# A mixer of two scans in rounds: one shared order of steps becomes a list for each engine

## The reference, cut to what matters

```python
def step(S, inp):                       # RWKV, in each head
    w_t, k_t, v_t, kk_t, a_t = inp[:5]
    sa = jnp.einsum('bhvk,bhk->bhv', S, kk_t)
    S = (S * w_t[:, :, None, :] - sa[..., None] * (kk_t * a_t)[:, :, None, :]
         + v_t[..., None] * k_t[:, :, None, :])
    ...
g = jnp.cumsum(lf_c, axis=2)            # HGRN, in chunks
inter = jnp.einsum('bhtk,bhkv->bhtv', q_c * jnp.exp(g), S)
...
mixed = concat(pool, rwkv, hgrn) * silu(gates);  out = layer_norm(ALPHA * x + gate * (mixed @ w_out))
```

## Time and profile before

| | us |
|---|---|
| median of 3 executions | 1521.52 |
| lowest, highest | 1518.86, 1522.16 |
| the profiled execution: its own time | 1515.97 |
| its span in the trace | 1514.1 |
| tail's last product to the block's last product | 189.1 to 507.6 |

### The profile page before, as it was taken

The page is one execution under the profiler, slowest core; times in us unless marked ns, Lnnn a source line. Parts: engine busy times, 40 slices in busy tenths (PEclk is TensorE's granted clock), DMA queues, the critical chain, the costliest instruction groups (busy, mean ns, idle before and its releaser), DMA issues.

```text
span 1514.1 us, 31114 instructions
## 1 busy us (share of the span) xinstructions
PE 1436.9 (95%) x13535; PEld 1289.6 (85%) x13535; DVE 825.7 (55%) x1495; ACT 332.2 (22%) x688; POOL 281.1 (19%) x144
## 2 busy tenths in 40 slices
PE   5999988997979899999999999999999999999998
PEld 2777877876868798998888999999999888899986
DVE  2345366557353467667435666534767743566643
ACT  1104034235332420143300120002014330012100
POOL 3403210000000047743100000003874310000000
PEclk8899999998999999999999999999999999999999
DMA  9533011102011454433344444445443334444451
GB/s 360 183 112 111 1 31 31 29 4 57 2 59 57 141 191 156 168 112 112 112 167 154 156 172 171 171 140 176 171 167 112 112 112 167 154 156 172 160 183 53
DMA packets 107479, 191.30 MB, mean 126 GB/s; under 512 B 8744, under 2 KB 25856, under 8 KB 107216
## 3 DMA queue, kind: packets, MB, share of 16 engines
q1 hardware_dynamic: 105968, 187.39, 35.3%
q10 hardware_dynamic: 448, 0.66, 0.3%
q0 software_dynamic: 928, 1.26, 0.2%
HBM read 187.32 MB, written 1.05 MB: 124 GB/s over the span
## 4 chain that ended last, share of the span: by engine, by line
PE 87%; DVE 3%; DMA 2%; issue 2%; DVEq 2%; ACT 1%; POOLq 1%; ACTq 1%; POOL 0%; SPq 0%
PE psum L1486 17%; PE psum L1347 14%; PE psum L1322 12%; PE psum L1483 6%; PE psum L1625 5%; PE psum L1606 4%; PE psum L1343 3%; PE psum L900 3%; PE psum L1538 2%; PE psum L974 2%; PE psum L983 2%; PE psum L1142 2%; PE psum L1198 2%; DMA arena<-in_mod_w 1%; PE psum L1407 1%
## 5 line engine op out<-in xcount | busy, mean ns | idle before, releaser
L1347 PE MATMUL psum<-arena 128*128 128x128 f32 x2240 | 262.9, 277 | 2.5 <-DVE arena L2652 1.3
L1347 PEld LDWEIGHTS psum<-arena 128*128 128x128 f32 x2240 | 255.6, 193 | 11.4 <-issue 8.0
L2057 ACT ACTIVATE arena<-psum 128x512 f32<-128x512 f32 (+5 forms) x248 | 118.3, 493 | 662.1 <-PE psum L1347 109.3
L1486 PEld LDWEIGHTS psum<-arena 128*128 128x128 f32 x2240 | 250.4, 192 | 0.1
L1486 PE MATMUL psum<-arena 128*128 128x128 f32 x2240 | 250.5, 275 | 0.0
L1322 PE MATMUL psum<-arena 128*128 128x256 f32 x896 | 195.6, 379 | 0.0
L1322 PEld LDWEIGHTS psum<-arena 128*128 128x128 f32 x896 | 169.5, 190 | 24.4 <-issue 0.3
L855 POOL TENSOR_TENSOR arena<-arena 128x1024 f32<-128x1024 f32 x12 | 28.4, 2371 | 376.6 <-DMA arena<-in_w_in 359.6
L1483 PE MATMUL psum<-arena 128*128 128x256 f32 x448 | 97.0, 379 | 0.0
L1483 PEld LDWEIGHTS psum<-arena 128*128 128x128 f32 x448 | 85.1, 190 | 11.6
L1625 PE MATMUL psum<-arena 128*128 128x256 f32 x336 | 73.5, 380 | 1.1 <-issue 1.1
(11 more groups left out here) (403 smaller groups left out, 2032.8 us busy)
## 6 DMA issues: line engine op xcount, KB each, us to landing
arena<-in_w_in SPq DMA_DIRECT2D x31, 2048.0 KB, 8.2
arena<-in_w_up SPq DMA_DIRECT2D x16, 2048.0 KB, 8.3
arena<-in_w_down SPq DMA_DIRECT2D x16, 2048.0 KB, 7.8
arena<-in_w_out SPq DMA_DIRECT2D x6, 2048.0 KB, 7.7
arena<-in_w_branch SPq DMA_DIRECT2D x6, 2048.0 KB, 7.9
arena<-in_mod_w SPq DMA_DIRECT2D x5, 2048.0 KB, 14.7
arena<-in_w_in SPq DMA_DIRECT2D x12, 512.0 KB, 4.0
arena<-in_w_in SPq DMA_DIRECT2D x3, 1024.0 KB, 6.6
```

The lines of the kernel that those rows point to most:

```text
L1347: mm = pe.matmul(b[:, n * P:(n + 1) * P], left[:, k, n * P:(n + 1) * P], right[:, k, :], start=k == 0, stop=k == half - 1)
L1486: mm = pe.matmul(b[:, n * P:(n + 1) * P], left[:, k, n * P:(n + 1) * P], right[:, k, :], start=first and n == 0 and k == 0, stop=last and ...
L2057: return act.activation(dst, src, ACT.Copy, scale=scale)
```

## The change

`TAIL` and `ROUNDS` go. Each engine gets a list of its own (`ORDERS`, keys P, A and D for TensorE, ScalarE and VectorE), all with the same steps of each stream but interleaved differently. Banks are still given out in TensorE's order; the counts by which an emptied bank is recognised follow the order of the engine that empties it. With it:

- Streams are cut finer: E has 11 steps (the running sums of a direction are two steps), C 12 (u and s apart), G 32 (two k-tiles of a gate tile in each), H 15, V 7.
- In the lists of rounds 0 and 1, VectorE's running sums of the next turn (E.2 to E.5) stand behind the copies of inverse levels 4 to 6, ScalarE's Ln of the key norm behind level 4's first step and its Exp behind level 5's (before, both behind level 6).
- HGRN's whole turn j is done in round j (before, its steps 2 to 7 were done in the chain part of round j-1).
- N and Q have two turns instead of three, heads (0, 1) together and head 2 alone. Both are out of rounds 0 and 1.
- The gate tiles are copied, not passed through Silu; Silu is applied to 128x1024 at once in a stream of its own, Z, at the start of rounds 1 and 2.
- ScalarE copies of levels 1 to 5 only the half of each i product that is used (128x256 for 128x512).
- The inner squares of `xf` are copied at the start of level 6's first step.
- M runs over the tiles in two parts, (2, 3, 5, 6) and then (0, 1, 7), each over all output columns.

```diff
-TAIL = "TTETETEEEEETEETTTHTTTTHE"
-ROUNDS = ("SHSHSHILHVIHVILHVIHVILHVIHLHIEHIEHIEHIEHIEIEECGECGHCGHCGEHCGHCGHCGHCGY",
-          "SSSILHIHILHIHILHIHLIEQNIEQNHIEQNHIEIEQNIEQNEQNCGECGHCGHCGEHCGHCGHCGHCGY",
-          "SSSILHQIHQILHQQIHQILHQIHLIQNIQNIQNIQNQNIQNIMCMCMCMCMCMCMCMCMYMNNMNMNNMMMMN")
+ORDERS = {
+    "P": ("TTETETEEEEEETEETTTHTTTTE",
+          "SSSIHLILHILILHIEHIHEHIVHIHVHIVHIVHIHIHVCVVGGCGCGGHCGCGCGGCGCGCGGCGCGCGEEEEEEEEEY",
+          "SSSIZHLILIHLILHIEHIHEIHIHIHHIHIHIHCGGCGCGGHCGCGCGGHCGCGCGGHCGCGCGEEEEEEEEEY",
+          "SSSIZHLILIHLILHIHINHIQQQHINNHIHHIHIHIQQQNNNHCCMCMHCMCMCHHCMCMCMCMCQQQCYQQQNMMNNMMMNNMMMN"),
+    "A": ("TTETETEEEEEETEETTTHTTTTE",
+          "SSSIHILLHIILLHIEHIHEHIEEEEEVHIHVHIEVHIVHIHIHVCCCVVGGGGGHECCCGGGGECCCGGGGCCCGGGEY",
+          "SSSIZHILLIHILLHIEHIHEIEEEEEHIHIEHHIHIHIHCCCGGGGGHECCCGGGGEHCCCGGGGHCCCGGGEY",
+          "SSSIZHILLIHILLHIQHINHINQQHINHIQNHHIHIQNHIQNHCCCMMHCCCMMHHCCCQMMMCCCMQQQYQQNNMMMMMMMMNNNN"),
+    "D": ("TTETETEEEEEETEETTTHTTTTE",
+          "SSSIHLILHILILHIEHIHEHIVHIHVHEIEVHIVHEIEHIHVCVVCCGGGGGHEECCCGGGGECCCGGGGECCCGGGEY",
+          "SSSIZHLILIHLILHIEHIHEIHIHEIEHHIHEIEHIHCCCGGGGGHEECCCGGGGHECCCGGGGHECCCGGGEY",
+          "SSSIZHLILIHLILHIHIQNHIHINNQQHIHHIHIHIQQQNNNHCCCMMHCCCMMHHCCCQMMMCCCMQQYQQQNNNMMMMMMMMNNN"),
+}
...
+def run_streams(engine, **streams):
+
+    for x, _, _ in order_of_streams(engine):
         next(streams[x])
...
         def inverse_scalar(act, j, copy, done, emptied):
...
                     rw.wait_filled(act, g)
-                    emptied(rw, copy(wh[r, d].rearrange("p u t -> p (u t)"), bank(rw, g)[r]))
+                    if l < 6:
+                        emptied(rw, copy(halves_of(wh[:, d].rearrange("p u t -> p (u t)"), l, d == 0), halves_of(bank(rw, g), l, d == 0)))
+                    else:
+                        emptied(rw, copy(wh[r, d].rearrange("p u t -> p (u t)"), bank(rw, g)[r]))
...
+        def gates_made(act, done):
+
+            for j in range(JT - 1):
+                v = hz[:, j:j + 4:3, :]
+                act.drain()
+                act.activation(v, v, ACT.Silu)
+                done("gates_ready")
+                yield
...
                 dve.tensor_tensor(km[:, d, :], km[:, d, :], k, ALU.mult)
                 fence()
+                yield
                 dve.tensor_tensor(blocks_of(c), blocks_of(c), m.unsqueeze(2).to_broadcast([P, 4, P]), ALU.subtract)
...
+            for part, ks in enumerate(((2, 3, 5, 6), (0, 1, 7))):
+                for n in range(4):
                     w = use_chunk(pe, 12 + n // 2)
```

More of the change, by code:

```diff
@@ L220, in __init__ @@
         self.met = met
+        for engine, order in emptied:
+            for n, g in enumerate([g for g, e, _ in order if e == engine], 1):
+                self.empty[g] = (engine, n)
     def bank(self, g):
@@ L241, in wait_all, with order_of_streams @@
                 eng.wait_ge(self.emptied[e], self.met[e])
[L244 to L254 removed]
+TURNS = {"T": 1, "V": 1, "M": 1, "G": JT - 1, "Z": JT - 1, "Q": 2, "N": 2}
+ORDERS = {
[12 more added lines that the diff above has]
+}
+def order_of_streams(engine):
+    steps, met = [], collections.Counter()
+    for x in "".join(ORDERS[engine]):
         n = len(GROUPS[x])
@@ L917, in prepare_tensor @@
             yield
-            for _ in range(6):
+            for _ in range(8):
                 yield
@@ L1183, in mixed_out_tensor @@
         def mixed_out_tensor(pe):
-            for n in range(4):
-                if n % 2 == 0:
+            for part, ks in enumerate(((2, 3, 5, 6), (0, 1, 7))):
+                for n in range(4):
                     w = use_chunk(pe, 12 + n // 2)
[L1188 to L1196, removed]
+                    if part:
+                        pe.wait_ge(sem("o_mixed"), 2)
+                    elif n == 0:
+                        ep.wait_all(pe)
+                        pe.wait_ge(sem("o_mixed"), 1)
+                        pe.wait_ge(sem("y_mixed"), 1)
+                    elif n == 2:
+                        hg.wait_all(pe)
+                    b = bank(wo, f"wo{n}")
+                    for t in range(2):
+                        c = (2 * (n % 2) + t) * P
                         for k in ks:
-                            pe.matmul(b[:, t * T:(t + 1) * T], w[:, k, c:c + P], mixed[k], start=k == 0 and t == 0, stop=False,
+                            pe.matmul(b[:, t * T:(t + 1) * T], w[:, k, c:c + P], mixed[k], start=k == 2 and t == 0, stop=False,
                                       skip_group_check=True)
@@ L1307, in turns_of, with two_turns_of @@
                 yield from stream(args[0], j, *args[1:])
+        def two_turns_of(stream, *args):
+            for js in ((0, 1), (2,)):
+                yield from stream(args[0], js, *args[1:])
         def layer_tensor(pe, l, take_bank, turn):
@@ L1875, in prepare_scalar @@
             done("e_gates")
-            yield
-            yield
-            yield
+            for _ in range(5):
+                yield
             ep.wait_filled(act, f"kk_{j}")
@@ L2038, in hgrn_scalar @@
             emptied(hg, copy(ktok.rearrange("p d c t -> p (d c t)"), bank(hg, f"ktok_{j}")))
-            for _ in range(5):
+            for _ in range(7):
                 yield
@@ L2452, in inverse_vector @@
             for l in range(1, 7):
+                if l == 6:
+                    if j == 0:
+                        dve.wait_ge(sem("squares_zeroed"), 1)
+                    for d in range(2):
+                        for r in HALVES:
+                            dve.tensor_copy(xf[r, d, :, r], xh[r, d])
                 yield
```

205 lines of the change are left out of this document (114 added, 91 removed).

## The result

The changed kernel is slower. Its median is 1532.9 us against 1517.0 us for the kernel before (20 executions each); the ratio is 1.0092, 95% interval 1.0069 to 1.0114, that is 14 us (the medians differ by 15.9). The forecast was 1516.9 us, 0.30% faster than the 1521.5 that three executions of the kernel before had given; its 20 executions here lie 4.5 us lower, so it is the direction and the difference that count, not the 1516.9. Slower by over 0.2% had a chance of 0.20. The profiled execution has a span of 1531.8 us (before 1514.1) and took 1533.67.

The account below looks back on a forecast made before the run. PE's queue was taken to bound the kernel. Old idle 34.0 + clock 10.8 + matmuls saved 0.9 - new idle 32.8 - new clock loss 8.3 = 4.6 us faster, giving 1516.9 us; range 1505 to 1526.

Parts of the forecast that it names:

- the clock: Time lost to PE's low clock in the rounds of the new kernel, put at 8.3 us.
- PE's new idle time: PE's idle time in the rounds: 10.8, 12.5 and 9.5 us in rounds 0, 1 and 2, in all 32.8.
- kk: The key norm's matmul in rounds 0 and 1, said to wait 0.86 us for ScalarE to empty a bank.
- the price of the sums: Running sums in rounds 0 and 1: PE waits of 4.6 and 7.1 us, plus 6.8 us of clock.
- I followed the three new lists against each other: How new idle time in the rounds was worked out, with durations from the profile rows; 32.8 us in all.
- The queue of 17.8 us has no gap.: VectorE's queue in round 1 from HGRN's level 1, without pause, against PE's 11.0 us; PE waits 7.1.
- the old idle time of 34.0 was all set free: In the rounds, all 34.0 us of PE's old idle time was counted as going.
- two stretches are sure, at 3.4 us each: Low clock behind the waits of 4.6 and 4.7 us; half a chance of another 3.0 behind round 2's 2.2.
- Rival 2: Waits of 1.6 to 2.2 us close together also take the clock down in the rounds; 1525.4 us, chance 0.17.
- Rival 1: Sums in rounds 0 and 1 are hidden and the clock holds; 1500.8 us, or 1505.5 with half the waits; chance 0.20.
- Rival 3: Sums only change places, waits behind them add up to what they were; 0.9 us faster, 1520.6; chance 0.19.
- Rival 4: ScalarE's half copies in the inverse levels save nothing; 0.4 to 1 us more, inside the forecast; no chance given.

Follow-up runs that it names:

- experiment 1: Changed kernel with VectorE's running sums moved behind the chain's state copies in rounds 0 and 1; 1516.3 us, ratio 0.9986 to the kernel before.
- experiment 11: Experiment 8's kernel with the four running-sum steps of VectorE put back where the changed kernel has them; 1525.3 us, ratio 1.0048 to the kernel before.
- experiment 2: Changed kernel with VectorE's growth behind the cross block put ahead of the output block's steps 2 and 3 in round 2; 1526.3 us, ratio 1.0053.
- experiment 5: Changed kernel with HGRN's state step of round 1 behind x of inverse level 5, on TensorE and VectorE; 1527.9 us, ratio 1.0065 to the kernel before.
- the repetition: The changed kernel again, unchanged, in one profiled execution; 1532.16 us.
- experiment 4: Changed kernel, order unchanged, with matmuls of constants that nobody reads put into TensorE's four long waits; 1526.3 us, ratio 1.0065 to the kernel before.
- experiment 3: Changed kernel with the edits of experiment 1 and experiment 2 together; 1511.8 us, ratio 0.9951 to the kernel before.
- experiment 6: Experiment 3's kernel with ScalarE copying all of each i product again instead of the used half; 1511.8 us, ratio 0.9946 to the kernel before.
- experiment 8: Experiment 3's kernel with three more moves: HGRN's level 0 (round 0), variance product (round 2), ScalarE's first decays (round 1); 1507.3 us, ratio 0.9920.
- experiment 7: Changed kernel with the running sums moved behind the chain's first copies in round 0 alone; 1520.6 us, ratio 1.0019 to the kernel before.

## Why the prediction was wrong, step by step

Two terms of the sum failed: the clock, put at 8.3 us and 18.7 in the trace, and PE's new idle time, put at 32.8 and 42.5.

**Held.** The waits at the cross block (4.6, measured 5.43), at level 5 (4.7, 4.79), at level 2 (0.75, 0.77), at the diagonal block of round 2 (2.2, 1.84), at HGRN's level 0 of round 0 (1.6, 1.64), at kk (0.86 twice), at yvar (1.7, 1.60) and at M's first product (1.1, 1.38); the half copy (384 ns, measured 385); u of round 1 no longer waits. The chain parts of rounds 0 and 1 have no idle time (0.3 each). The balance as a method held too: the 9.7 and 10.4 us that the two terms are off make 20.1, the whole distance between the 4.6 us forecast faster and the 15.5 by which the rounds are longer.

**Held in size: the price of the sums.** The forecast had 4.6 + 7.1 us of waits and 6.8 of clock at them, 18.5 us; experiments 1 and 11 measure 16.6 and 18.0 for their place alone. There is luck in how near that is: the waits came out longer (5.43 for 4.6, 9.5 for 7.1), but moving the sums made a new one, so that idle time in the rounds fell by 11.9 us in experiment 1's trace. That price was in the sum. It ended on the wrong side because the rest of the change was taken to bring 23 us and brought 2 or 3, which cannot be told apart from nothing (experiment 1 beside the kernel before, 0.9957 to 1.0015). The two failed terms show there too: without the sums' waits the forecast is 21.1 us of idle time and 1.5 of lost clock, and experiment 1's trace has 30.6 and 16.6.

**Failed: "I followed the three new lists against each other"** for the chain part of round 2, which was given 2.3 us and idles 5.5. I took VectorE's second and third step of M as free; they stand ahead of the growth for which o waits. Experiment 2: 6.6 us, 2.4 of it the wait (3.43 to 1.00).

**Failed: "The queue of 17.8 us has no gap."** The second piece of round 1 (1.6) was 3.95, since the state needs the bank that VectorE empties behind the sums, and PE's standing there made VectorE pause 3.5 us. Experiment 5 took that out, 2.7 us.

**Failed: the old idle time of 34.0 was all set free.** 10.4 us of it are waits to which the trace gives no releaser ("issue"), some inside a run of 64 equal matmuls, the 2.91 of the earlier trace rows with them; my walk through the new lists had no such term, and the new trace has 5.7 us of them (4.9 of it here, PE's waits, 188 to 523 us; columns: total, times, longest):

```profile
PE psum L1309 <- DVEq L3032: 3.4, 1, 3.4
PE psum L992 <- DVE arena L2490: 2.9, 6, 1.1
PE psum L1001 <- issue: 2.9, 4, 1.3
PE psum L992 <- issue: 2.0, 3, 1.2
```

These 5.7, the 3.4 of o and 2.4 at the state (3.95 for 1.6) are 11.5 us, against the 9.7 by which idle time was forecast too low; the terms that came out smaller make up the rest. What these waits are stays open. They differ between executions: 8.2 us in the repetition, which accounts for the 2.4 us more of idle time that it has.

**Failed: "two stretches are sure, at 3.4 us each", and half a chance of a third.** The largest single error, 10.4 us, and more a matter of number than of size. There were five falls, not 2.5, and at 17.7 us they cost 3.5 each, which is the forecast's price. Term by term: behind the two waits that were called sure 7.4 + 2.5 = 9.9 us for 6.8; at 434 us 1.7 for the 1.5 of the half chance; behind the state and o 1.8 + 4.3 = 6.1 us for nothing, since the forecast had these two waits at 1.6 and nought; and 1.0 that only the finer reckoning finds. So the two waits that the walk missed are paid for twice, 5.8 us as idle time and 6.1 as clock. The one size that was far off is the first: the forecast's price came from stretches of 4 to 7 us, and behind the wait of 5.43 the clock stayed at half for 17 us, in the repetition for 20. Nearly all of that lies in the busy part of the chain, where every microsecond at half clock costs one half. The Trainium skill ("TensorE: Matmul & The Clock Gate", Part 1) says that activity releases the clock; experiment 4 agrees in direction, its fillers took the clock's part from 32.1 to 18.4 us.

**Rivals.** Rival 2 (the clock falls oftener) came nearest, and its sign came true: half clock in five stretches, for the four or more that it asked for. Its mechanism did not: it wanted waits of 1.6 to 2.2 us close together, and of these only the one at 434 us had a fall, in the repetition not even that. Four of the five falls stand at waits of 3.4 us and more, two that the forecast had and two that it had too short or not at all. Rival 1 is what experiment 3 makes of the order, by another way: its 1505.5 us against 1511.8; its guess that the clock stays up below waits of some 2.5 us does not hold, since it fell at 1.84 us. Rival 3 is out: the idle time is 42.5 us, not 34, and moving the sums away gives 16.6 us. Rival 4 asked for 0.4 to 1 us, too little for the times to tell; by experiment 6's trace the half copies save PE 1.1 us of waits.

What stays open: why the clock falls in one execution and not in another with the same waits, why it fell in experiment 1 with waits of 0.4 us ahead of it, what the "issue" waits are, and some 4.5 us of experiment 4. Which of the other parts of the change gives the 0.5 to 0.8% by which experiments 3 and 8 beat the kernel before was not taken apart.

## What to carry to other kernels

Follow an engine's queue with the other's banks in hand: a pause of one engine makes the next pause of the other, so a sum of queue entries is a lower bound. When a wait is only moved, ask what it costs where it lands; here 5 us ahead of a chain part cost some 12 (experiment 7), 7 of them as clock, which fell for the dense work behind it. Count idle time whose cause the trace does not show apart from the rest before calling it a gain, and judge the clock by the mean of many executions, not by one trace.

## What the runs showed of the hardware

In the twelve traces of the changed kernel and its variants, PE stands in the rounds 21 times for 3.4 to 5.5 us (the cross block, the state, level 5, o), and each time the granted clock is at half behind it. HGRN's diagonal block in round 2 waits 1.84 us in eleven of them, and the clock falls there in four. A wait of 3.47 or 3.48 us behind the rounds (in the changed kernel at 535 us), the same in all thirteen traces, that of the kernel before with them, has a fall in ten. And in experiment 1 the clock fell with nothing longer than 0.4 us just ahead. So a long wait makes a fall likely, and how likely depends on more than its length.

Between two executions of one kernel with waits equal to 0.01 us the low stretches differ (3.4 us or none at 434 us, 10 or 7 us at o). The clock's part of the span scatters by 3 to 7 us (standard deviation) in each kernel, what is left by 2.3 to 4.6, and over the executions of the changed kernel span and clock's part have a correlation of 0.85: most of the scatter of 1520 to 1540 us is the clock. It is kept up longer by matmuls that nobody reads: with 13.1 of 18.7 us of waits filled, the clock's part fell by 13.7 us.
